# Block 2 of a hybrid transformer kernel: raw attention scores as three rounded products instead of one fp32 product

## The chip, the cores and the metric

The kernel runs on one core of one Trainium2 chip. The metric is the device time of one execution in microseconds (us). A core has a matrix engine (TensorE, PE in the rows, with its weight loads as PEld), a vector engine (VectorE, DVE), an activation engine (ScalarE, ACT), and a queue of DMA issues (SyncE, SP). Each works through its own list of instructions in order; they wait for each other by semaphores.

## The reference, cut to what matters

Four layers work on 512 tokens of width 1024 (`DEPTH = 2` layers of a first kind, then 2 of a second kind, "block 2"). Only block 2 is touched. Its layer is: one input projection, four groups of attention of four heads each with head width 64, an output projection, a layer norm, a gated feed-forward network, a layer norm. The four groups are

```python
out_a = _causal_softmax_blocks(fq, fk, fv, HEAD_DIM ** -0.5, cum)   # "FOX": causal, with a forget bias
out_b = _mla(cq, ckv, kr, ...)                                      # "MLA": q.k of 64 plus a rotary part of 32
out_c = _stick_breaking_blocks(sq, sk, sv)                          # "SB"
out_d = _swa_sink_alibi(wq, wk, wv, sinks, slopes)                  # "SWA": window of 128 keys
```

and each begins with raw scores s = q k^T over 64 channels, in fp32. These raw scores are all that the change is about.

## The kernel before, in words

**Data types.** A projection is not made with fp32 products. Each operand t is kept as a high part (t rounded to the type fp32r, made by a copy) and a rest (t minus the high part, again in fp32r), and a product is three rounded products, high x high, high x rest, rest x high, added up in PSUM: `mm3`, lines 583 to 587. ScalarE makes the high part of each weight unit (L1090), VectorE the rest (L1102). The raw scores of block 2 are the exception: their operands are plain fp32 tiles, and each is one fp32 product.

**The attention stage of block 2** has 32 steps in each of the two layers. Eight units of two heads follow each other (SWA, SWA, MLA, MLA, SB, SB, FOX, FOX), and each has four steps. Step s is unit a = s div 4, block qb = s mod 4. The two heads of a unit lie in one tile of 128 partitions, head 0 in partitions 0 to 63 and head 1 in 64 to 127. The names of the tiles are a letter for the kind (w, u, s, f for SWA, MLA, SB, FOX), q, k or v, and a number. `DEST` (L828) says where each lies.

**PE in step s**: the raw scores of step s (`scores`, L1932, product on L1943; for SB `sb_scores_of`, L1987, product on L1997), then weights times values of step s-2 (L1984, L2026), the transposes of the probabilities of step s-1 (L1968), and as filling the projection of later tiles in pieces of one eighth (`fill`, two halves a step; its order is `QUOTA`). In SB steps the running sums (L2012, L2015) stand in the place of the transposes, behind the first half of the filling. In step 8 (`FILL_FIRST`) the first half of the filling comes ahead of the scores. From step 28 on the scores are issued one step ahead. In the first step of a unit `operands_wait` (L1903) waits for the unit's q and k tiles. The number of key columns in one product is 128, 256, 384 and 512 in the four steps of a unit, in SWA 128, 256, 256 and 256.

**ACT in step s**: it copies the finished projection tiles out of PSUM (`tile_copy`, L2233), does what is due of v tiles and of norms (`rstd`, L2247, L2249), then the exponentials, then the copy of the transposed probabilities (L2279), and last the casts of weight units (`casts_of`, L1090).

**DVE in step s**: the row maxima (L761), the rests of weight units (L1102), the running sums of SB (L2610 to L2662), rotations (L2550 to L2552), the normalised query latents (L2568 to L2571, `query_latents`; the first in step 3, after `normalise`), `normalise` (L2537 to L2544), in step 7 the split of the rotated query (L2563, L2564), and in some steps a group norm or the sum of squares.

**When q and k tiles end.** A projection tile ends in the half step in which its last eighth is done (`ENDS`): wq1 in the second half of step 2, uq0 in the first half of 5, uk0 in the first half of 6, sq0 in the second of 7, uq1 and uk1 in the first of 8, sk0 in the second of 10, sq1 in the second of 14, sk1 in the second of 16, fq0 in the first of 19, fk0 in the second of 20, fq1 in the first of 23, fk1 in the second of 24. wq0 and wk are made ahead of step 0.

**DMA.** SP loads the weight units and, for MLA, exchanges halves of the rotary tiles (L956); the rotation of the query on DVE in step 7 (L2550) waits for these.

Of the kernel before, what the change touches and what calls it, by code (L numbers as in the profile page):

```python
# [35 lines left out]
SEQ = 512  # L36
# [72 lines left out]
class Steps:  # L109
# [10 lines left out]
    def wait(self, value=None):  # L120
# [12 lines left out]
          "sb_ln": 16, "sb_soft": 16, "sb_low": 12, "sb_cum": 16, "sb_sum": 12, "sb_prob": 16, "gate_ln": 1, "gate_ready": 1,  # L133
# [16 lines left out]
def program(nc, x_in, pos_in, const_in, mask_in, swa_in, rope2_in, col_in, w_in, row1_in,  # L150
            row2_in, out):
    ctx = ExitStack()
    with ctx:
# [110 lines left out]

        ps = [ctx.enter_context(nc.psum_tensor(f"bank{i}", [P, SEQ], F32)) for i in range(8)]
# [108 lines left out]
        gate_ln = sem("gate_ln")  # L374
        gate_in = sem("gate_in")
# [444 lines left out]
        def stacked(a, qb):  # L820
# [13 lines left out]
                "fv0": raw_t[0], "fv1": raw_t[1]}  # L834

# [1029 lines left out]
        def tensor_block2(pe, layer):  # L1865
# [67 lines left out]
            def scores(a, qb):  # L1933
# [4 lines left out]
                q, k = DEST[q_name(a)], DEST[k_name(a)]  # L1938
# [49 lines left out]
            def sb_scores_of(a, j):  # L1988
# [5 lines left out]
                q, k, S = DEST[q_name(a)], DEST[k_name(a)], banks(a, j)  # L1994
# [200 lines left out]
        def scalar_block2(act, st, layer):  # L2195
# [39 lines left out]

            def v_copy(name):
# [92 lines left out]
            for name in FIRST:  # L2329
                tile_copy(name)  # L2330
                next_cast(name)
            for step in range(STEPS):
                a, qb = divmod(step, NB)
                ended = ENDS.get((step - 1, 1), [])
                tiles_out(ended)
                late = LATE.get(step - 1, "")
# [35 lines left out]
                casts_of((*ended, *ENDS[step, 0]))  # L2372
            pT_copy(N_ATT - 1, NB - 1)
# [108 lines left out]
        def vector_block2(dve, st, layer):  # L2482
# [197 lines left out]

            for name in FIRST:
                next_split(name)
            for step in range(STEPS):
# [61 lines left out]
                if step == GATE_STEP + 1:  # L2745
                    gate_sums()
                if step == TAIL:
# [338 lines left out]
```

## Time and profile before

| | |
|---|---|
| Median of 3 runs | 2331.2 us (2330.55 to 2332.4) |
| Profiled execution, its own time | 2330.97 us |
| Its span from the first to the last instruction | 2329.2 us |
| Busy share of the span: PE, PEld, DVE, ACT | 99%, 81%, 63%, 42% |
| Granted clock of PE, mean | 0.999 |
| Chain that ended last, by engine | PE 98%, DVE 1%, ACT 1% |
| Attention stage of block 2, step 0 to the end of the scores of step 31 | about 1134.5 to 1316 us, and 1738 to 1920 us |

The chain of waits goes back from the last instruction to whatever released it. It gives a piece the time from the end of the piece before it, so a line of it is the time that the piece really took of the span, while the duration of a single matmul record holds the latency of a pipelined instruction. Matmuls on the same line that follow each other are one piece with their count. An fp32 product has two records, a rounded product has one, so a pair of heads in fp32 is "x4".

### The profile page before, as it was taken

How to read it: one execution, taken by the hardware profiler on the slowest of the kernel's cores; microseconds unless marked ns; L12 is line 12 of the kernel's file. 1: busy time of each engine (PE TensorE's matmuls, PEld its weight loads, DVE VectorE, ACT ScalarE, POOL GpSimd, SP SyncE). 2: the span in 40 equal slices, each digit the busy share in tenths (PEclk: the TensorE clock that was granted, in tenths of full speed). 3: DMA queues.
4: the chain of work that ended last, by engine and by line, in shares of the span. 5: the costliest groups of instructions: out<-in, count | busy, mean ns of one | idle time of the engine just before them, and what ended most of it. 6: DMA issues, size and time to landing. Idle time of an engine off the chain costs nothing.

```text
span 2329.2 us, 30258 instructions
## 1 busy us (share of the span) xinstructions
PE 2317.0 (99%) x11444; PEld 1879.2 (81%) x11444; DVE 1478.3 (63%) x2773; ACT 983.4 (42%) x1853; POOL 0.2 (0%) x4
## 2 busy tenths in 40 slices
PE   9999999999999999999999999999999999999998
PEld 7888888888888888888877788888887768888887
DVE  6788764345578774334577668567566767658565
ACT  5356542223446643222566533133246664323222
POOL 0000000000000000000000000000000000000000
PEclk9999999999999999999999999999999999999999
DMA  5333333332243333233231232324303112422322
GB/s 175 108 105 105 103 100 91 99 104 87 91 116 106 104 93 123 92 100 109 66 86 55 64 129 90 127 64 136 127 31 94 55 46 100 145 82 91 128 72 90
DMA packets 73583, 226.32 MB, mean 97 GB/s; under 512 B 14240, under 2 KB 15136, under 8 KB 72672
## 3 DMA queue, kind: packets, MB, share of 16 engines
q1 hardware_dynamic: 73296, 224.13, 30.9%
q8 instruction: 92, 1.51, 0.3%
q14 instruction: 51, 0.42, 0.1%
q10 hardware_dynamic: 144, 0.26, 0.0%
HBM read 204.83 MB, written 2.10 MB: 89 GB/s over the span
## 4 chain that ended last, share of the span: by engine, by line
PE 98%; DVE 1%; ACT 1%; DMA 0%; issue 0%; DVEq 0%
PE bank L585 26%; PE bank L587 25%; PE bank L586 25%; PE bank L2162 2%; PE bank L2161 2%; PE bank L2160 2%; PE bank L1256 2%; PE bank L1984 1%; PE bank L1943 1%; PE bank L1243 1%; PE bank L1968 1%; PE bank L519 1%; PE bank L1233 1%; PE bank L1231 1%; PE bank L1997 1%; PE bank L2026 0%
## 5 line engine op out<-in xcount | busy, mean ns | idle before, releaser
L585 PE MATMUL bank<-h_hi,w_hi 128*128 128x512 f32 x1984 | 787.7, 397 | 0.4 <-DVE w_lo L1102 0.2
L587 PE MATMUL bank<-h_lo,w_hi 128*128 128x512 f32 x1984 | 774.0, 390 | 0.0
L586 PE MATMUL bank<-h_hi,w_lo 128*128 128x512 f32 x1984 | 773.7, 390 | 0.0
L585 PEld LDWEIGHTS bank<-h_hi,w_hi 128*128 128x128 f32 x1984 | 373.0, 188 | 81.3 <-issue 7.5
L587 PEld LDWEIGHTS bank<-h_lo,w_hi 128*128 128x128 f32 x1984 | 372.5, 188 | 79.4
L586 PEld LDWEIGHTS bank<-h_hi,w_lo 128*128 128x128 f32 x1984 | 373.3, 188 | 71.4 <-issue 0.2
L1102 DVE TENSOR_TENSOR w_lo<-raw_w,w_hi 128x1024 fp32r<-128x1024 f32 x314 | 379.1, 1222 | 76.3 <-ACT w_hi L1090 73.2
L1090 ACT ACTIVATE w_hi<-raw_w 128x1024 fp32r<-128x1024 f32 x314 | 327.6, 1055 | 140.6 <-DMA raw_w<-w_dram 140.4
L2392 ACT ACTIVATE nrm<-bank 128x512 f32<-128x512 f32 x44 | 26.3, 599 | 288.7 <-PE bank L587 288.7
L1545 ACT ACTIVATE ext<-bank 128x512 f32<-128x512 f32 x48 | 28.7, 598 | 281.1 <-PE bank L587 281.1
L1845 DVE TENSOR_TENSOR rope_a<-ext,bank 128x512 f32<-128x512 f32 x32 | 22.0, 688 | 160.9 <-PE bank L587 107.4
L2160 PE MATMUL bank<-seven_hi,y_hi 128*128 128x512 f32 x252 | 98.1, 389 | 0.0
L2161 PE MATMUL bank<-seven_hi,y_lo 128*128 128x512 f32 x252 | 98.1, 389 | 0.0
L1489 ACT ACTIVATE prob<-prob,small 128x128 f32<-128x128 f32 (+3 forms) x128 | 70.9, 556 | 55.7 <-DVE small L761 55.7
L2774 DVE TENSOR_TENSOR ytmp<-nrm,bank 128x512 f32<-128x512 f32 x26 | 17.9, 687 | 117.3 <-PE bank L587 117.2
L585 PE MATMUL bank<-act_hi,w_hi 128*128 128x512 f32 x212 | 83.1, 392 | 0.0
L587 PE MATMUL bank<-act_lo,w_hi 128*128 128x512 f32 x212 | 82.6, 390 | 0.0
L586 PE MATMUL bank<-act_hi,w_lo 128*128 128x512 f32 x212 | 82.5, 389 | 0.0
L761 DVE CUSTOM_DVE_ANT_0 prob<-bank,causal 128x128 f32<-128x128 f32 (+3 forms) x112 | 49.4, 479 | 45.9 <-PE bank L1233 20.0
L2774 DVE TENSOR_TENSOR y_raw<-nrm,bank 128x512 f32<-128x512 f32 x18 | 12.4, 688 | 91.1 <-PE bank L587 91.1
L1502 ACT ACTIVATE pT<-bank 128x128 f32<-128x128 f32 (+3 forms) x96 | 38.2, 432 | 73.9 <-PE bank L1243 73.9
L2842 DVE SCALAR_TENSOR_TENSOR x<-x,bank 128x512 f32<-128x512 f32 x84 | 54.9, 686 | 20.8 <-PE bank L2162 20.8
(369 smaller groups left out, 3517.3 us busy)
## 6 DMA issues: line engine op xcount, KB each, us to landing
raw_w<-w_dram SPq DMA_DIRECT2D x312, 512.0 KB, 3.6
down_raw<-w_dram SPq DMA_DIRECT2D x36, 512.0 KB, 4.4
extra_raw<-w_dram SPq DMA_DIRECT2D x10, 512.0 KB, 4.6
k_lo<-k_lo SPq DMA_DIRECT2D x32, 128.0 KB, 2.3
ln_row<-row_dram SPq DMA_DIRECT2D x4, 1024.0 KB, 6.1
last_raw<-w_dram SPq DMA_DIRECT2D x8, 512.0 KB, 4.5
x<-x_dram SPq DMA_DIRECT2D x4, 512.0 KB, 6.9
rowp<-row_dram SPq DMA_DIRECT2D x2, 1024.0 KB, 9.1
```

What stands on the lines that cost most here:

```text
L585: nc.tensor.matmul(dst, lh, rh, start=start, stop=False)
L586: nc.tensor.matmul(dst, ll, rh, start=False, stop=False)
L587: return nc.tensor.matmul(dst, lh, rl, start=False, stop=stop)
L761: return nc.vector.tensor_tensor_reduce(out=to, in0=bank, in1=mask, scale=-1.0, scalar=3.0e38, op0=ALU.add, op1=ALU.min, accum_out=low)
L1090: nc.scalar.activation(hi_of(u), raw_of(u), ACT.Copy).then_inc(hi_cast, 1)
L1102: nc.vector.tensor_tensor(lo_of(u), raw_of(u), hi_of(u).bitcast(F32), ALU.subtract) \
L1256: last = nc.tensor.matmul(O[rows, cols], vs[a % 2][:, b, rows], pT[ti1(a, qb, m) % 2][:, b * P:(b + 1) * P], start=(b == 0), stop=(b == qb))
L1489: nc.scalar.activation(prob[m][:, 0:nk], prob[m][:, 0:nk], ACT.Exp, scale=-1.0, bias=small[:, 24 + 2 * qb + m:25 + 2 * qb + m], accum_out= ...
L2160: nc.tensor.matmul(bank[t][:, :], y_hi[:, p, a, y], high, start=begin, stop=False, skip_group_check=True)
L2161: nc.tensor.matmul(bank[t][:, :], y_lo[:, p, a, y], high, start=False, stop=False, skip_group_check=True)
L2162: made = nc.tensor.matmul(bank[t][:, :], y_hi[:, p, a, y], low, start=False, stop=p == PAIRS - 1, skip_group_check=True)
L2842: nc.vector.scalar_tensor_tensor(out=part, in0=part, scalar=scale, in1=bank[t][:, :], op0=ALU.mult, op1=sign).then_inc(down_added, 1)
```

## The change

Each q and k tile of the raw scores, in its place as fp32, gets a high part in another buffer (`HEAD_HIGH`) by a copy on ScalarE (`head_cast`), and its rest, written over the fp32 tile itself, by a subtraction on VectorE (`head_rest`). PE then makes three rounded products for each head, with the heads alternating. The casts stand at the end of an ACT step; for wq1 right behind the copy of the tile at the head of step 3. The rests stand at the end of the DVE step after the one in which the cast is due; for wq1 at the end of the same step 3. `operands_wait` also waits for the later one of the two rests.

```diff
+        HEAD_HIGH = {"wq0": act_hi[:, 0, :], "wk": act_hi[:, 1, :], "wq1": act_hi[:, 2, :], "uq0": act_lo[:, 7, :],
+                     "uk0": act_lo[:, 11, :], "sq0": spare[:, :], "uq1": act_hi[:, 8, :], "uk1": act_hi[:, 9, :],
+                     "sk0": act_hi[:, 10, :], "sq1": act_lo[:, 10, :], "sk1": act_lo[:, 11, :], "fq0": act_hi[:, 8, :],
+                     "fk0": act_hi[:, 9, :], "fq1": act_lo[:, 8, :], "fk1": act_lo[:, 9, :]}
...
+        HEAD_TURN = {name: i + 1 for i, name in enumerate(HEAD_HIGH)}
@@ tensor_block2
             def operands_wait(a):
                 tile_wait(q_name(a))
                 tile_wait(k_name(a))
+                if q_name(a) in HEAD_HIGH:
+                    pe.wait_ge(head_low, at(head_low, max(HEAD_TURN[q_name(a)], HEAD_TURN[k_name(a)])))
...
-                for m in range(2):
-                    bank_wait(a, qb, m)
-                    rows = slice(HD * m, HD * m + HD)
-                    last = nc.tensor.matmul(S[m][:, 0:nk], q[rows, block_q], k[rows, k0:k1], start=True, stop=(kind == SWA))
-                    if kind == SWA:
-                        last.then_inc(scores_ready, 1)
+                for i, (q, k) in enumerate(((q_hi, k_hi), (q_hi, k_low), (q_low, k_hi))):
+                    for m in range(2):
+                        if i == 0:
+                            bank_wait(a, qb, m)
+                        rows = slice(HD * m, HD * m + HD)
+                        last = nc.tensor.matmul(S[m][:, 0:nk], q[rows, block_q], k[rows, k0:k1],
+                                                start=(i == 0), stop=(kind == SWA and i == 2))
+                        if kind == SWA and i == 2:
+                            last.then_inc(scores_ready, 1)
...
-                for m in range(2):
-                    rows = slice(HD * m, HD * m + HD)
-                    nc.tensor.matmul(S[m][:, lo:SEQ], k[rows, lo:lo + P], q[rows, lo:SEQ], start=True, stop=True) \
-                      .then_inc(sb_scores, 1)
+                for i, (q, k) in enumerate(((q_hi, k_hi), (q_low, k_hi), (q_hi, k_low))):
+                    for m in range(2):
+                        rows = slice(HD * m, HD * m + HD)
+                        last = nc.tensor.matmul(S[m][:, lo:SEQ], k[rows, lo:lo + P], q[rows, lo:SEQ], start=(i == 0), stop=(i == 2))
+                        if i == 2:
+                            last.then_inc(sb_scores, 1)
@@ scalar_block2
+            def head_cast(name):
+                t = TILE[name]
+                if name in HEAD_HIGH:
+                    act.wait_ge(tile_out[t % 2], at(tile_out[t % 2], t // 2 + 1))
+                    nc.scalar.activation(HEAD_HIGH[name], DEST[name][:, :], ACT.Copy).then_inc(head_high, 1)
...
             for name in FIRST:
                 tile_copy(name)
+                head_cast(name)
                 next_cast(name)
...
                 tiles_out(ended)
+                if "wq1" in ended:
+                    head_cast("wq1")
...
                 casts_of((*ended, *ENDS[step, 0]))
+                for name in (*ended, *ENDS[step, 0]):
+                    if name != "wq1":
+                        head_cast(name)
@@ vector_block2
+            def head_rest(name):
+                if name in HEAD_HIGH:
+                    dve.wait_ge(head_high, at(head_high, HEAD_TURN[name]))
+                    nc.vector.tensor_tensor(head_parts(name)[1], DEST[name][:, :], HEAD_HIGH[name].bitcast(F32), ALU.subtract) \
+                      .then_inc(head_low, 1)
...
             for name in FIRST:
                 next_split(name)
+                head_rest(name)
...
                     gate_sums()
+                for name in (*ENDS.get((step - 2, 1), []), *ENDS.get((step - 1, 0), []), *ended):
+                    if (name == "wq1") == (name in ended):
+                        head_rest(name)
```

`head_parts(name)` is the pair of the high part and the rest. The biases that are added to the scores in PSUM (L1949, L1954, L1959) and all else are left as they are.

## Rows read from the trace of the kernel before

**Rows 1.** The page: busy time by engine, and the last chain by engine.
```profile
PE 2317.0 (99%) x11444; PEld 1879.2 (81%) x11444; DVE 1478.3 (63%) x2773; ACT 983.4 (42%) x1853; POOL 0.2 (0%) x4
...
PE 98%; DVE 1%; ACT 1%; DMA 0%; issue 0%; DVEq 0%
```

**Rows 2.** Lines L1943 and L1997: durations in ns, starts, forms.
```profile
L1943 PE MATMUL bank<-ks,qs x128: 271/482/694, 1188.1 to 1918.6; 64*128 64x128 f32 x32, 64*128 64x256 f32 x32, 64*128 64x384 f32 x32, 64*128 64x512 f32 x32
...
L1943 PE MATMUL bank<-wk_t,wq_t x64: 271/377/481, 1134.5 to 1784.5; 64*128 64x256 f32 x48, 64*128 64x128 f32 x16
...
L1997 PE MATMUL bank<-wq_t,wk_t x32: 272/482/694, 1230.1 to 1854.1; 64*128 64x128 f32 x8, 64*128 64x256 f32 x8, 64*128 64x384 f32 x8, 64*128 64x512 f32 x8
...
L1997 PE MATMUL bank<-cq_t,ckv_t x32: 271/482/694, 1257.4 to 1882.2; 64*128 64x128 f32 x8, 64*128 64x256 f32 x8, 64*128 64x384 f32 x8, 64*128 64x512 f32 x8
```

**Rows 3.** Chain of waits, raw scores of 256, 128, 384, 512 columns: start, us, piece.
```profile
1180.42 0.63 PE bank L1943 x4
...
1188.16 0.42 PE bank L1943 x4
...
1196.65 0.85 PE bank L1943 x4
...
1202.50 1.06 PE bank L1943 x4
```

**Rows 4.** Chain of waits, two rounded bias products: 128, 256, 384, 512 columns.
```profile
1285.60 0.37 PE bank L1949 x2
...
1291.98 0.43 PE bank L1949 x2
...
1297.39 0.55 PE bank L1949 x2
...
1302.72 0.66 PE bank L1949 x2
```

**Rows 5.** Chain of waits, rounded products of block 1: 128, 256, 384, 512 columns.
```profile
110.29 0.22 PE bank L1233 x2
...
113.53 0.24 PE bank L1233 x2
...
119.71 0.36 PE bank L1233 x2
...
126.47 0.45 PE bank L1233 x2
```

**Rows 6.** Step 3 into 4, first layer: timelines of ACT, DVE; PE's chain.
```profile
1155.51 0.60 ACT L2247 ACTIVATE sz<-bank 128x512 f32<-128x512 f32 x1 [0.26 <-PE bank L1900]
...
1163.21 0.69 DVE L2571 TENSOR_TENSOR act_lo<-ytmp,act_hi 128x512 fp32r<-128x512 f32 x1
...
1162.77 0.42 PE bank L1943 x4
```

**Rows 7.** Step 7 into 8, both layers: timeline of DVE; PE's chain.
```profile
1184.73 0.69 DVE L2550 TENSOR_TENSOR rope_a<-raw_t,cos 128x512 f32<-128x512 f32 x1 [2.19 <-DMA nrm<-raw_t]
...
1189.31 0.69 DVE L2564 TENSOR_TENSOR act_lo<-qr_t,act_lo 128x512 fp32r<-128x512 f32 x1
...
1792.18 0.69 DVE L2564 TENSOR_TENSOR act_lo<-qr_t,act_lo 128x512 fp32r<-128x512 f32 x1
...
1792.02 0.42 PE bank L1943 x4
```

**Rows 8.** Steps 19 to 23, first layer: window of step 19; DVE's timeline; PE's chain.
```profile
1249.90:1257.50 7.60, 7.60 (x38) 5.38 (x40) 7.36 (x19) 6.41 (x12) 0.00 (x0) 1.00 0.22 69
...
1273.62 0.43 DVE L2662 TENSOR_TENSOR sp_low<-pn,act_hi 128x256 fp32r<-128x256 f32 x1
...
1274.99 0.29 PE bank L2012 x2
...
1281.65 0.56 DVE L2662 TENSOR_TENSOR sp_low<-ext,act_hi 128x384 fp32r<-128x384 f32 x1
...
1282.50 0.37 PE bank L2012 x2
```

More of the change, by code:

```diff
@@ L132 @@
           "pv_done": 32, "o_out": 8, "sq_ready": 6, "sq_parts": 5, "rs_ready": 6, "y_ready": 8, "sb_scores": 16, "sb_masked": 16,
-          "sb_ln": 16, "sb_soft": 16, "sb_low": 12, "sb_cum": 16, "sb_sum": 12, "sb_prob": 16, "gate_ln": 1, "gate_ready": 1,
+          "sb_ln": 16, "sb_soft": 16, "sb_low": 12, "sb_cum": 16, "sb_sum": 12, "sb_prob": 16, "gate_ln": 1, "gate_ready": 1, "head_high": 15, "head_low": 15,
           "latent_ready": 3, "gu_ready": END_TILES, "pair_ready": 2 * PAIRS * SEVEN_PARTS, "down_done": 14 * SEVEN_PARTS,
@@ L263, in program @@
         last_hi = [sb(f"last_hi{i}", [P, UNIT], F32R, at=at[1]) for i, at in enumerate(last_at)]
+        head_rests = {name: sb(f"{name}_rest", [P, SEQ], F32R, at=addr[name])
+                      for name in ("wq_t0", "wq_t1", "wk_t", "ckv_t", "cq_t0", "qs0", "qs1", "ks0", "ks1")}
         ps = [ctx.enter_context(nc.psum_tensor(f"bank{i}", [P, SEQ], F32)) for i in range(8)]
@@ L374, in program @@
         gate_ln = sem("gate_ln")
+        head_high = sem("head_high")
+        head_low = sem("head_low")
         gate_in = sem("gate_in")
@@ L834, in program, with head_parts @@
                 "fv0": raw_t[0], "fv1": raw_t[1]}
+        HEAD_HIGH = {"wq0": act_hi[:, 0, :], "wk": act_hi[:, 1, :], "wq1": act_hi[:, 2, :], "uq0": act_lo[:, 7, :],
+                     "uk0": act_lo[:, 11, :], "sq0": spare[:, :], "uq1": act_hi[:, 8, :], "uk1": act_hi[:, 9, :],
+                     "sk0": act_hi[:, 10, :], "sq1": act_lo[:, 10, :], "sk1": act_lo[:, 11, :], "fq0": act_hi[:, 8, :],
+                     "fk0": act_hi[:, 9, :], "fq1": act_lo[:, 8, :], "fk1": act_lo[:, 9, :]}
+        HEAD_HOME = {"wq0": "wq_t0", "wk": "wk_t", "wq1": "wq_t1", "uq0": "qs0", "uk0": "ks0",
+                     "sq0": "wq_t0", "uq1": "qs1", "uk1": "ks1", "sk0": "wk_t", "sq1": "cq_t0",
+                     "sk1": "ckv_t", "fq0": "qs0", "fk0": "ks0", "fq1": "qs1", "fk1": "ks1"}
+        HEAD_TURN = {name: i + 1 for i, name in enumerate(HEAD_HIGH)}
+        def head_parts(name):
+            return HEAD_HIGH[name], head_rests[HEAD_HOME[name]][:, :]
         def q_name(a):
@@ L1937, in scores @@
                     operands_wait(a)
[L1938 removed]
+                (q_hi, q_low), (k_hi, k_low) = head_parts(q_name(a)), head_parts(k_name(a))
                 S = banks(a, qb)
[L1940 to L1945 removed]
+                for i, (q, k) in enumerate(((q_hi, k_hi), (q_hi, k_low), (q_low, k_hi))):
[7 more added lines that the diff above has]
+                            last.then_inc(scores_ready, 1)
                 for m in range(2):
@@ L1993, in sb_scores_of @@
                 bank_wait(a, j, 0)
-                q, k, S = DEST[q_name(a)], DEST[k_name(a)], banks(a, j)
-                for m in range(2):
-                    rows = slice(HD * m, HD * m + HD)
-                    nc.tensor.matmul(S[m][:, lo:SEQ], k[rows, lo:lo + P], q[rows, lo:SEQ], start=True, stop=True) \
-                      .then_inc(sb_scores, 1)
+                (q_hi, q_low), (k_hi, k_low), S = head_parts(q_name(a)), head_parts(k_name(a)), banks(a, j)
+                for i, (q, k) in enumerate(((q_hi, k_hi), (q_low, k_hi), (q_hi, k_low))):
[4 more added lines that the diff above has]
+                            last.then_inc(sb_scores, 1)
             def sb_between(a, j):
```

## The prediction
> **What bounds the kernel now.** I read the page first: PE is busy 99% of the span, and the chain that ended last is 98% PE [rows 1]. So whatever PE no longer does is gained one for one, and every time PE has to wait for a new thing is lost one for one; there is no slack on PE in which a wait could hide. DVE and ACT have slack on average, and the average says nothing here: what matters is whether DVE has finished at the moments at which PE asks. So I next read the scores' lines for how many products there are [rows 2], the chain of waits for what a pair of heads takes of the span [rows 3], and the timelines of DVE and ACT around the starts of units for when a rest could be ready [rows 6 to 8].
>
> **Part 1: the products on PE.** Counting records [rows 2] and dividing by 4 (two heads, two records each), both layers hold 16 pairs of 128 columns, 24 of 256, 12 of 384 and 12 of 512, 64 in all. They take 0.42, 0.63, 0.85 and 1.06 us [rows 3]. That is 0.21 us of lead-in and then 0.21 us for each 128 columns of both heads together. By the durations of the records [rows 2] each head of a pair of 512 columns needs some 0.85 us by itself, so the heads already run side by side in fp32, and this is not what the change brings.
>
> The three rounded pairs do not occur in this trace on half the rows. The nearest rows are two rounded products one after the other behind a change of the array's shape: 0.37, 0.43, 0.55 and 0.66 us [rows 4], lead-in included. A third one costs half of the rows for pairs in block 1, 0.11, 0.12, 0.18 and 0.225 us [rows 5]. If the two heads run side by side as they do in fp32, three pairs are therefore 0.48, 0.55, 0.73 and 0.885 us. The differences are +0.06, -0.08, -0.12 and -0.175 us, so 16 x 0.06 - 24 x 0.08 - 12 x 0.12 - 12 x 0.175 = **-4.5 us**. At 128 columns it is a loss, since a rounded product of 128 columns is no faster than 0.11 us. Bounds: if they do not overlap at all, each pair has three more products of 0.11 to 0.225 us, 16 x 0.33 + 24 x 0.36 + 12 x 0.54 + 12 x 0.675 = +28.5 us, so +24 us in place of -4.5. In the other direction, if the lead-in of about 0.2 us went away, 64 x 0.2 = 12.8 us more would be gained. I take -4.5, as side by side is what this trace shows of tiles of this shape.
>
> The skill bears on this twice. The Trainium skill, TensorEngine Tiling (Array Packing), Key Properties, says that different tiles load and multiply in parallel, and that a change of tiling mode drains the engine: that speaks for the overlap and for the lead-in staying. Against the full overlap stands the Trainium skill, TensorE: Matmul & The Clock Gate, Part 3, where four tiles packed by rows gave 3.07 times, not four times. With a loss of that proportion the sum would be higher by an estimated 8 us; the fp32 pairs of this trace show no such loss.
>
> **Part 2: the casts and rests.** 15 tiles in each of 2 layers give 30 casts on ACT and 30 rests on DVE. A rest is a 128x512 subtraction like L2571, 0.69 us [rows 6], 21 us of DVE in all; a cast is about as long as L2247, 0.60 us [rows 6], 18 us of ACT. Most of it lies beside PE's work. The casts of wq0 and wk, and their rests, are done about 1.3 us ahead of the scores of step 0. The rests of sq0, sk0, uq1, uk1, sq1, sk1, fq0 to fk1 are issued one to seven steps ahead of their use, so these waits cost nothing in themselves. Two rests have no step between them and their use, and these are the price of the change.
>
> **wq1, step 3 into 4.** Its rest is at the end of DVE's step 3, behind `query_latents(0)`, whose last instruction starts at 1163.21 and lasts 0.69 us, until 1163.9. PE begins the scores of step 4 at 1162.77 [rows 6], so DVE is already 1.1 us behind PE there; nobody waited for it before. The cast on ACT sits ahead of L2247, in an idle time of 0.26 us [rows 6]; it takes 0.5 us of issue and so moves ACT by 0.26, and with it the cast of a weight unit and all of DVE's step behind that. The rest ends at 1163.93 + 0.26 + 0.69 = 1164.9. PE stands for 2.1 us, in both layers: +4.2 us. Behind the waiting scores on PE are the weights times values of step 2, the transposes and the filling, all ready and all held up, as PE is in order.
>
> **uk0, step 7 into 8.** Its rest is at the end of DVE's step 7, behind the rotation of the query (which waits for a DMA until 1184.73), a weight unit's rest, `normalise` and the query's split. The last of these starts at 1189.31 and 1792.18; the next could start 0.61 us later and lasts 0.69, so it ends at 1190.6 and 1793.5. PE wants to start the scores of step 8 at 1188.16 [rows 3] and 1792.02 [rows 7]. That is 2.5 and 1.5 us, and PE comes 0.16 us earlier in each layer from its savings in steps 6 and 7, while the DMA keeps its time: +4.3 us. The cast of uk0 is done several us before. The rest of uq0, at the end of step 6, falls into DVE's idle time of 2.19 us ahead of the rotation [rows 7] and costs nothing. The three rests at the end of step 9 come when PE has been put back by 2 us, and are absorbed.
>
> **Steps 18 to 23, SB.** Here DVE has nearly no idle time: 7.36 of 7.6 us in step 19 [rows 8]. The casts of sk1 (ACT's step 17) and the rests of sk1, fq0 and fk0 (DVE's steps 18, 20, 22) put it back by 0.5 + 0.6 + 0.6 us before it next catches up. PE needs the low parts of SB's sums: the second of step 21 ends at 1274.05 and is used at 1274.99, that of step 22 ends at 1282.2 and is used at 1282.50 [rows 8]. Slack is 0.9 and 0.3 us, so 1.7 us of delay costs some 1.1 us at the first and 0.5 at the second, 1.6 us a layer; the second layer's DVE has a quarter us more of idle time. Bounds are 0 and 1.6 us; I take 1.2 a layer, nearer to the worked end, **+2.4 us**.
>
> **Sum:** -4.5 + 4.2 + 4.3 + 2.4 = +6.4 us. The profiled execution took 2330.97 us, which gives 2337.4; the median of the runs is 0.2 us above it, so 2337.5 us. A measurement of this kernel can tell about 0.2%, 4.7 us, from no change.
>
> **The rivals.**
> - *The SB stretch absorbs its rests.* PE's own savings or idle time of DVE that I have not seen hide them; only the waits for wq1 and uk0 are paid. 2331.0 - 4.5 + 8.5 = 2335.1 us, no change that can be told. For it: DVE's late times there were worked out through a long chain. Against: the slack of 0.3 us [rows 8]. 0.20.
> - *The two waits are not paid*, since DVE comes earlier than I worked out: 2331.2 - 4.5 = 2326.7, on the edge of faster. Against it: in both layers DVE is late already [rows 6, 7]. 0.06.
> - *The lead-in goes away (faster).* Rounded operands of the scores let PE load their weights beneath the projection product ahead of them, at the head of each of the 64 groups. Then 2337.5 - 12.8 = 2324.7 us. It decides from 0.18 us a group: 11 us bring it below 2326.5. Against it: the rounded products behind a change of shape pay about 0.2 us as well (0.66 us for two of 0.225) [rows 4, 5]. 0.06.
> - *Heads overlap only in part.* A loss of 0.04 us for each of the 192 rounded pairs is 8 us: 2345.5 us. The record of fp32 speaks against it [rows 3]. It is the packing figure of the Trainium skill, TensorE: Matmul & The Clock Gate, Part 3. 0.08.
> - *Rounded products of two heads don't overlap at all.* 2337.5 + 28.5 = 2366 us. Nothing in this trace shows rounded products on half the rows. 0.08.
> - *The change doesn't do what it says* is little of a rival here, as the instructions are counted; it would be that three rounded pairs take what two fp32 records took, with the waits paid: 2331.2 + 10.9 = 2342.1. 0.04.
>
> **How the numbers follow.** My forecast, 2337.5 us, has 0.48; its own range is 2334.5 to 2341. The cases from 2335.1 to 2345.5 hold 0.80 together; the range runs from 2331 (taking in that both the waits and the SB stretch cost less) to 2345. Slower by over 0.2% (above 2335.9) is most of the forecast and the three dearer cases: 0.42 + 0.08 + 0.08 + 0.04 = 0.62. Within 0.2%: the first rival, the forecast's lower end and half of the second: 0.29. Faster: 0.09.
>
> **What would show it.** In the profile after, the score groups in the chain should read x6 and 0.48, 0.55, 0.73 and 0.89 us. PE should have a wait of 2.1 us on `head_rest` ahead of step 4's scores in each layer, and of 2.7 and 1.7 us ahead of step 8's, and these should be the longest waits of PE. L2012 should be released by DVE's L2662 in steps 22 and 23. PE's busy time should fall a little, and DVE's and ACT's rise by some 20 us each. I am wrong if the groups are above 1 us at 256 columns (no overlap), if the two waits are under 1 us, or if PE's idle time is elsewhere.

## The result, and the profile after

| | before | after |
|---|---|---|
| Median of the runs | 2331.61 us (2330.55 to 2332.4, 4 runs) | 2344.91 us (2341.99 to 2347.39, 4 runs) |
| Ratio | | 1.0058, 95% interval 1.0046 to 1.007 |
| Profiled execution, its own time | 2330.97 us | 2347.39 us |
| Its span | 2329.2 us | 2345.6 us |
| Granted clock of PE, mean | 0.999 | 0.996 |

The changed kernel is slower by 13.3 us. The forecast was 6.3 us slower, 2337.5 us, in a range that ended at 2345.0: the sign is right and the median just inside, but the size is wrong by more than a factor of two. That the median lies inside is luck: no case on which the range was built holds what makes up the difference. The profiled execution is the slowest of the four, by 2.5 us over the median; why will be seen below.

The page of the kernel after, busy time by engine and the last chain by engine (against [rows 1]):

```profile
PE 2321.6 (99%) x11572; PEld 1892.3 (81%) x11572; DVE 1496.7 (64%) x2803; ACT 999.1 (43%) x1883; POOL 0.2 (0%) x4
...
PE 92%; DVE 4%; ACT 2%; issue 1%; SPq 1%; DMA 1%; DVEq 0%; ACTq 0%
```

DVE has 30 instructions and 18.4 us more, ACT 30 and 15.7 us more. PE's share of the last chain has gone from 98% to 92%. PE's busy time has risen by 4.6 us, although each large group has become shorter. That is the first sign of something that the forecast does not contain.

The chain of waits of the kernel after, raw scores of 256, 384, 512 and 128 columns (against [rows 3]):

```profile
1147.79 0.55 PE bank L1965 x6
...
1205.09 0.72 PE bank L1965 x6
...
1210.81 0.89 PE bank L1965 x6
...
1216.98 0.48 PE bank L1965 x6
```

Forecast were 0.55, 0.73, 0.885 and 0.48 us. The products cost what was worked out.

PE's waits in the kernel after: total us, times, longest. All that stands here is new; in the same view of the kernel before, no wait lies on a line of the raw scores or of SB's sums.

```profile
PE bank L1965 <- DVE wq_t_rest L2721: 4.7, 2, 2.4
PE bank L1965 <- issue: 2.6, 1, 2.6
PE bank L1965 <- ACT ks L2258: 2.0, 1, 2.0
...
PE bank L2037 <- DVE sp_low L2699: 0.7, 4, 0.2
...
PE bank L1991 <- DVE pn L2581: 0.6, 1, 0.6
```

L1965 is the raw scores' product, L2721 the rest. The first row is the wait for wq1's rest ahead of step 4, in both layers. The second and third are the waits ahead of step 8. "ACT ks" had been copied long before, so this is a case in which the view names the wrong releaser; the timelines of DVE and PE show the right one:

```profile
1163.52 0.69 DVE L2608 TENSOR_TENSOR act_lo<-ytmp,act_hi 128x512 fp32r<-128x512 f32 x1
1164.25 0.69 DVE L2721 TENSOR_TENSOR wq_t_rest<-wq_t,act_hi 128x512 fp32r<-128x512 f32 x1
...
1165.20 0.33 PE L1965 MATMUL bank<-act_hi 64*128 64x128 f32 x2 [2.35 <-DVE wq_t_rest L2721]
...
1194.25 0.68 DVE L2721 TENSOR_TENSOR ks_rest<-ks,act_lo 128x512 fp32r<-128x512 f32 x1
...
1195.14 0.33 PE L1965 MATMUL bank<-act_lo 64*128 64x128 f32 x2 [1.97 <-ACT ks L2258]
```

The rest of wq1 ends at 1164.94, the forecast said 1164.9; PE goes on 0.26 us later, which the forecast had left out. The rest of uk0 ends at 1194.93, and PE goes on at 1195.14.

What follows each of the four waits is the surprise. The windows of the kernel after, 3.3 or 3.4 us each, which begin 0.4 to 2.2 us after PE has gone on (columns: us; busy time of PE, PEld, DVE, ACT, POOL; PEclk, the granted clock; DMA share; GB/s):

```profile
1166.50:1169.90 3.40, 3.40 (x11) 2.83 (x10) 3.24 (x7) 1.56 (x8) 0.00 (x0) 0.51 0.00 0
1197.30:1200.60 3.30, 3.30 (x12) 2.16 (x11) 2.26 (x6) 3.30 (x8) 0.00 (x0) 0.50 0.54 120
1777.50:1780.90 3.40, 3.40 (x20) 2.70 (x19) 3.00 (x10) 1.97 (x8) 0.00 (x0) 0.51 0.04 16
1808.20:1811.60 3.40, 3.40 (x15) 2.68 (x12) 2.02 (x10) 3.06 (x9) 0.00 (x0) 0.51 0.33 80
```

The same place in the kernel before, where PE had not waited:

```profile
1162.80:1166.20 3.40, 3.40 (x25) 2.77 (x26) 3.19 (x11) 3.39 (x11) 0.00 (x0) 1.00 0.50 154
```

PE's clock falls from 2.4 to 1.2 GHz for some 3.4 us behind each wait. PE counts as fully busy in these windows, so no view of waits shows the loss. The chain shows it as twice the price of the same product:

```profile
1153.64 0.23 PE bank L591
...
1168.55 0.42 PE bank L590
1168.98 0.43 PE bank L591
1169.40 0.43 PE bank L592
```

To follow where the time goes, I took from the timelines when the scores of a step begin, relative to the scores of step 0 of the first layer, and the difference to the kernel before. A rise from one row to the next is time lost there. The columns of the runs are explained with them; "again" is a second profile of the changed kernel.

```
layer, step  after  again  E3 both  E4 all  E9 fp32  E10 cast
1       3    -0.11  -0.11   -0.11   -0.11    0.00    -0.11
1       4     2.23   2.23   -0.19   -0.19    0.00    -0.19
1       5     3.91   3.85   -0.13   -0.13    0.00    -0.13
1       7     4.09   4.08    0.09    0.09    0.29    -0.32
1       8     6.78   7.05    0.35    0.63    0.47     0.57
1       9     8.02   7.11    0.41    0.69    0.72     0.63
1      22     7.43   6.20   -0.52   -0.39    0.83    -0.42
1      24     8.69   7.46    0.73   -0.20    0.87    -0.24
1      31     8.22   6.99    0.25   -0.67    0.86    -0.71
2       3     7.95   6.77    0.02   -0.91    0.87    -0.95
2       4    10.29   9.11   -0.07   -0.99    0.87    -1.03
2       5    11.87   9.15   -0.01   -0.93    0.87    -0.97
2       7    12.07   9.35    0.17   -0.71    1.17    -1.16
2       8    14.73  11.97    0.13   -0.76    1.17    -1.20
2       9    16.34  13.60    0.19   -0.70    1.17    -1.14
2      22    15.54  12.83   -0.61   -1.64    1.17    -2.09
2      24    16.77  14.04    0.59   -1.47    1.13    -1.92
2      31    16.30  13.57    0.12   -1.94    1.13    -2.39
```

In the column "after" each wait shows as two steps: the wait itself (2.34 us from step 3 to 4, 2.69 us from 7 to 8), and then 1.68, 1.24, 1.58 and 1.61 us in the step behind it, 6.1 us in all. Between steps 22 and 24, SB, 1.26 and 1.23 us are lost. Elsewhere the shift falls slowly, which is the saving of the products.

### The profile page after: what moved, and what is told of

Read it like the earlier page. It is cut to its first block, busy times and chain, and to the rows that moved or that the text cites. A ratio compares the mean times of both kernels' runs of the same rounds, so it can differ in the third digit from the quotient of the medians.

```text
span 2345.6 us, 30586 instructions
## 1 busy us (share of the span) xinstructions
PE 2321.6 (99%) x11572; PEld 1892.3 (81%) x11572; DVE 1496.7 (64%) x2803; ACT 999.1 (43%) x1883; POOL 0.2 (0%) x4
## 4 chain that ended last, share of the span: by engine, by line
PE 92%; DVE 4%; ACT 2%; issue 1%; SPq 1%; DMA 1%; DVEq 0%; ACTq 0%
PE bank L590 24%; PE bank L592 24%; PE bank L591 24%; PE bank L2187 2%; PE bank L2185 2%; PE bank L2186 2%; PE bank L1274 2%; PE bank L2007 1%; PE bank L1261 1%; PE bank L1991 1%; PE bank L1965 1%; PE bank L524 1%; PE bank L1251 1%; PE bank L1249 1%; DVE w_lo L1120 1%
```

## The experiments

The theory at this point, **C**: the forecast's steps are right, and what it lacks is a price for the half clock behind each of the two waits in each layer. The rival, **R**: the clock falls for the load of the added work and not for the waits; when a wait is taken away, its own length alone comes back.

**E1, the rest of wq1 forward,** right behind the row maxima of step 3:

```diff
                     row_max(a, qb, 1)
+                if "wq1" in ended:
+                    head_rest("wq1")
...
-                    if (name == "wq1") == (name in ended):
+                    if name not in ('wq1',) and (name == "wq1") == (name in ended):
```

> Only the rest of wq1 is moved, from the end of DVE's step 3 to right behind its two row maxima, where DVE stands idle for 2.7 us and the cast is long done. Theory C (a wait of PE costs its own length and, behind it, a stretch of 3.4 us at half clock, 1.7 us): 2344.9 - 2 x 2.35 - 2 x 1.7 = 2336.8 us, two stretches at a clock of 0.5 in place of four, none behind step 4. Rival R (the clock falls for the load of the added work and not for the waits; only the waits themselves come back): 2340.2 us, and the clock still falls near 1167 us. By both PE has no wait above 0.3 us ahead of step 4's scores.

Measured: 2338.45 us (8 runs), ratio 1.0029 [1.0018, 1.0039]. It lies between both expectations and decides nothing by itself. PE has no wait at step 4 any more; those at step 8 stay. The timeline of PE and the windows behind the two waits of this kernel:

```profile
1189.83 0.33 PE L1965 MATMUL bank<-act_lo 64*128 64x128 f32 x2 [1.82 <-ACT ks L2258]
...
1795.56 0.33 PE L1965 MATMUL bank<-act_lo 64*128 64x128 f32 x2 [2.03 <-ACT ks L2258]
```

```profile
1191.50:1194.80 3.30, 3.30 (x26) 2.31 (x27) 2.49 (x7) 3.30 (x11) 0.00 (x0) 1.00 0.46 104
1797.20:1800.50 3.30, 3.30 (x10) 2.37 (x9) 2.26 (x6) 3.26 (x11) 0.00 (x0) 0.50 0.43 83
```

In this profile the wait of the second layer has the half clock behind it, that of the first has not. So the price does not come with every wait; a single profile cannot give it.

**E2, the rest of uk0 forward,** in step 7 ahead of the query's rotation, that of wq1 as in the changed kernel:

```diff
+                if "uk0" in ENDS.get((step - 1, 0), []):
+                    head_rest("uk0")
                 if LATE.get(step - 2) == "cq":
                     query_latents(1)
```

> Only the rest of uk0 is moved, from the end of DVE's step 7 to ahead of the rotation of the query, where DVE waits 0.85 us for a DMA. Theory C: two waits of 2.6 us and two stretches at half clock go: 2344.9 - 5.2 - 3.4 = 2336.3 us, with no fall of the clock behind step 8. Rival R: 2339.7 us, the clock still falls near 1197 us.

Measured: 2339.66 us (4 runs), 1.0036 [1.0022, 1.005]: the time that R expected. But the fall of the clock near 1197 us that R expected too is not there; the profile shows C's mechanism with a size that C did not have. The waits at step 8 are gone, the two of 2.36 us at step 4 remain, and behind the first the clock is half for twice as long:

```profile
1165.30:1171.90 6.60, 6.60 (x28) 5.28 (x29) 4.69 (x14) 1.94 (x8) 0.00 (x0) 0.50 0.05 22
1776.20:1779.50 3.30, 3.30 (x9) 2.52 (x9) 3.13 (x7) 1.11 (x6) 0.00 (x0) 0.50 0.00 0
```

From step 4 to 5 the long one costs 3.1 us (the shift, taken as in the table, goes from 2.23 to 5.35 us) and the short one 1.7 us (7.58 to 9.24).

**E3, both forward:**

> Both moves together. Theory C: 2344.9 - 4.7 - 5.2 - 6.8 = 2328.2 us, below the kernel before (2331.6), clock 0.999 as before, and only the SB stretch's late low parts (about 1.3 us a layer) left of the cost. Rival R: 2335.0 us, slower than before, clock 0.996.

Measured: 2331.58 us (11 runs), ratio 1.0000 [0.9991, 1.0009]. The two moves, of two subtractions of 0.69 us per layer, give back all that the change had cost: 13.3 us of median. There is no stretch of half clock in the attention stage, and PE has no wait on L1965, although every cast and rest is still made. R falls. C's time missed by 3.4 us: it took four stretches of 1.7 us off a median of executions that do not all have four (E11 below). What is still lost stands in the column "E3 both" of the table. Between steps 22 and 24 it loses 1.25 and 1.20 us, and from step 5 to 9 of the first layer 0.54 us.

**E4, the SB stretch relieved as well.** To test whether the first of these is the rests of sk1, fq0 and fk0, they stand between DVE's softplus sums, sk1 and fk0 ahead of the second, fq0 ahead of the first:

```diff
+                if "fq0" in ENDS.get((NB * a + j - 2, 0), []):
+                    head_rest("fq0")
                 for m in range(2):
+                    if m and "sk1" in ENDS.get((NB * a + j - 2, 1), []):
+                        head_rest("sk1")
+                    if m and "fk0" in ENDS.get((NB * a + j - 3, 1), []):
+                        head_rest("fk0")
                     dve.wait_ge(sb_ln, at(sb_ln, w + m + 1))
```

> As the one before, and in the SB steps the rests of sk1, fq0 and fk0 are moved from the ends of DVE's steps 18, 20 and 22 into places where it waited for ACT: between the two softplus sums of steps 18 and 23, and ahead of them in step 21. Theory S (these three rests made the low parts of the SB sums late): the loss of 1.3 us a layer at steps 22 to 24 goes, 2325.5 us. Rival (the late part comes from the casts on ACT in steps 17 and 19, or DVE is simply full): 2328 us, L2037 in the same wait.

Measured: 2329.02 us (11 runs), 0.999 [0.9981, 0.9999]. 2.6 us faster than E3, and 2.5 us faster than the kernel before. The steps 22 to 24 now lose 0.19 and 0.17 us. So the rests of SB cost 2.6 us with everything else equal. The second low part of steps 21 and 22 on DVE's timeline, E3 and then E4, against 1273.62 and 1281.65 us before [rows 8]:

```profile
1274.32 0.43 DVE L2699 TENSOR_TENSOR sp_low<-pn,act_hi 128x256 fp32r<-128x256 f32 x1
...
1282.35 0.56 DVE L2699 TENSOR_TENSOR sp_low<-ext,act_hi 128x384 fp32r<-128x384 f32 x1
```

```profile
1273.53 0.43 DVE L2705 TENSOR_TENSOR sp_low<-pn,act_hi 128x256 fp32r<-128x256 f32 x1
...
1281.56 0.56 DVE L2705 TENSOR_TENSOR sp_low<-ext,act_hi 128x384 fp32r<-128x384 f32 x1
```

In E3 they come 0.70 us late, in E4 0.09 us early. PE comes to step 22 of E3 0.5 us early, by its shorter products, and loses that and 0.7 us more. The view of waits shows two waits of 0.2 us there in the profile of E3, one in each layer, and two in that of E4 as well; the difference lies in gaps too short for the view. Three rests that PE asks for only steps later cost 1.3 us a layer, by what stands behind them in DVE's list. The time that theory S gave, 2325.5 us, stood on C's 2328.2 us for E3; its step of 2.6 us was right.

**E5, the wait covered instead of taken away.** The rest of wq1 stays late, but PE gets ready work ahead of the scores of step 4:

```diff
-                if step == FILL_FIRST:
+                if step in (4, FILL_FIRST):
...
-                if step != FILL_FIRST:
+                if step not in (4, FILL_FIRST):
```

> The changed kernel with every cast and rest where it was, but PE's filling of step 4 that stood behind that step's first scores is issued ahead of them (some 2.1 us of ready work against the wait of 2.35 us for the rest of wq1). Theory C (what the wait costs is PE standing still, plus a stretch at half clock behind it): PE's wait ahead of step 4's scores is 0.3 us or gone, no half clock behind it, and the time is near that of the kernel with wq1's rest moved forward, 2338.5 us (2337 to 2340.5). Rival R (the late rest puts back the chain of DVE and ACT behind it, so that filling in PE's gap only moves the gap into the steps after it): PE's idle time comes back in steps 4 to 6 and the time stays above 2342 us.

Measured: 2340.26 us (4 runs), 1.0038 [1.0023, 1.0053], inside C's range and 1.8 us above E1, whose waits at step 8 were shorter. PE waits 0.32 us instead of 2.35. The rows, waits at step 4 and twice at step 8, and the windows behind those at step 8:

```profile
1166.16 0.33 PE L1965 MATMUL bank<-act_hi 64*128 64x128 f32 x2 [0.32 <-DVE wq_t_rest L2721]
...
1192.08 0.33 PE L1965 MATMUL bank<-act_lo 64*128 64x128 f32 x2 [2.24 <-ACT ks L2258]
...
1798.52 0.33 PE L1965 MATMUL bank<-act_lo 64*128 64x128 f32 x2 [2.33 <-ACT ks L2258]
```

```profile
1193.80:1197.10 3.30, 3.30 (x26) 2.30 (x26) 2.53 (x7) 3.30 (x11) 0.00 (x0) 1.00 0.55 138
1798.80:1805.50 6.70, 6.70 (x35) 4.77 (x32) 3.33 (x11) 4.63 (x11) 0.00 (x0) 0.50 0.36 90
```

At the scores of step 5 this kernel is 0.24 us behind the kernel before, where the changed kernel is 3.91 behind. The rival, that the loss only moves into the steps behind, had 2342 us or more and falls. So the late rest by itself costs little; it is PE standing still that costs, and where PE did not stand, the clock stayed full. At step 8, the wait of 2.33 us had a long half clock behind it and the one of 2.24 us none.

**E6, the products undone, all else kept.** Raw scores as before's two fp32 products; the rests go over the high parts and nobody reads them:

```diff
-                for i, (q, k) in enumerate(((q_hi, k_hi), (q_hi, k_low), (q_low, k_hi))):
-                    for m in range(2):
...
+                for m in range(2):
+                    bank_wait(a, qb, m)
+                    rows = slice(HD * m, HD * m + HD)
+                    last = nc.tensor.matmul(S[m][:, 0:nk], q[rows, block_q], k[rows, k0:k1], start=True, stop=(kind == SWA))
...
-                    nc.vector.tensor_tensor(head_parts(name)[1], DEST[name][:, :], HEAD_HIGH[name].bitcast(F32), ALU.subtract) \
+                    nc.vector.tensor_tensor(HEAD_HIGH[name], DEST[name][:, :], HEAD_HIGH[name].bitcast(F32), ALU.subtract) \
```

> The changed kernel with all its casts, rests and waits, but the raw scores as the two fp32 products of before; the rests are written over the high parts and are read by nobody. It isolates the products. Theory P (three rounded pairs cost 0.48, 0.55, 0.72 and 0.89 us where fp32 costs 0.42, 0.63, 0.85 and 1.06): the waits of 2.35 and 2.6 us stay, the groups are those of before, and the time is that of the changed kernel, 2344.9 us, plus 4 to 5 us: 2349.3 us (2347.5 to 2351.5). Rival: the saving of the products is lost again elsewhere (PE only waits longer for DVE or the exchange), and the time is within 1.5 us of the changed kernel's.

Measured: 2347.31 us (4 runs), 1.0068 [1.0051, 1.0084], 16.1 us above the kernel before of the same chip, where the changed kernel was 13.3 above. The waits and the half clock are there with fp32 products too (2.27, 2.66, 2.27 and 1.32 us, the first three followed by half clock in this profile), so they do not belong to the rounded products. The saving comes out at 2.8 us instead of 4 to 5, between both expectations, but the number of half-clock stretches varies from run to run and blurs such a difference. E9 is the cleaner price.

**E7, the heads not in turn.** On E4: all three products of one head, then all three of the other.

```diff
-                for i, (q, k) in enumerate(((q_hi, k_hi), (q_hi, k_low), (q_low, k_hi))):
-                    for m in range(2):
+                for m in range(2):
+                    for i, (q, k) in enumerate(((q_hi, k_hi), (q_hi, k_low), (q_low, k_hi))):
```

> The fastest version so far (all five rests moved forward, 2329.0 us) with the three rounded products of one head ahead of the three of the other, in place of the two heads in turn. Theory 1 (only neighbours of different heads run side by side: of six products one pair overlaps, so a group takes two products more, 0.22, 0.24, 0.36 and 0.45 us): 16 x 0.22 + 24 x 0.24 + 12 x 0.36 + 12 x 0.45 = 19 us more, 2348 us (2344 to 2352). Theory 2 (PE takes the products of the second head beside the first's whatever their order): 2329 to 2331 us. Theory 3 (nothing overlaps): 28.5 us more, 2357.5 us.

Measured: 2329.12 us (10 runs), 0.9991 [0.9982, 1.0]. No difference to E4's 2329.02; theory 2 holds, and the alternation brings nothing. The timeline of PE of this kernel, a group of 128 columns, puts one product of each head (x2) at each start, although in the program the three of the first head come first:

```profile
1208.96 0.33 PE L1965 MATMUL bank<-act_hi 64*128 64x128 f32 x2
1209.12 0.28 PE L1965 MATMUL bank<-ks_rest,act_hi 64*128 64x128 f32 x2
1209.24 0.28 PE L1965 MATMUL bank<-act_hi,qs_rest 64*128 64x128 f32 x2
```

The trace has the second head's first product 10 ns behind the first head's first, not behind its third. The Trainium skill, TensorEngine Tiling (Array Packing), Key Properties, says that different tiles can load and multiply in parallel; the trace agrees, and adds that a tile does not wait for products that are ahead of it in the program but on the other rows. In all 64 groups of this profile the second head starts 10 ns behind the first. So "PE is in order", as the forecast has it, holds for the waiting scores and what stands behind them, and not between the two heads' products.

**E8, a shorter wait.** wq1's rest forward, uk0's rest between step 7's `normalise` and the query's split:

```diff
+                if "uk0" in ENDS.get((step - 1, 0), []):
+                    head_rest("uk0")
                 if ROTATE2.get(step - 1) == "qr":
                     dve.wait_ge(qk_ready, at(qk_ready, 2))
                     split_query()
```

> The rest of wq1 moved forward as before, that of uk0 only ahead of the query's split at the end of step 7, so that PE's wait for it ahead of step 8 is some 1.0 to 2.0 us in place of 2.0 to 2.7; none at step 4. Theory C (every such wait is followed by a stretch of half clock worth 1.6 us): 2331.6 + 2 x 1.5 + 2 x 1.6 = 2337.8 us. Rival L (a wait clearly shorter than 2 us leaves the clock full; in the runs so far waits of 2.35 and 2.7 us were always followed by half clock and one of 2.0 us was not): 2331.6 + 2 x 1.5 = 2334.6 us, and no stretch at half clock in the profile.

Measured: 2333.84 us (10 runs), 1.0013 [1.0003, 1.0022]. PE's waits at step 8:

```profile
1189.35 0.33 PE L1965 MATMUL bank<-act_lo 64*128 64x128 f32 x2 [0.93 <-ACT ks L2258]
...
1794.52 0.33 PE L1965 MATMUL bank<-act_lo 64*128 64x128 f32 x2 [1.41 <-issue]
```

No half clock in the profile, as L expected, and 2333.84 us is nearer to its 2334.6 than to C's 2337.8; E3 + 0.9 + 1.4 gives 2333.9. But of the ten runs seven lie between 2332.3 and 2333.9 us and three at 2336.0 to 2336.9, and two of these three have a mean clock of 0.998 where the others have 0.999. Only one run is profiled, so what these three did is not seen; a half-clock stretch would fit them. A wait of 1 to 1.4 us is cheaper; that it is safe is not shown.

**E9, the products priced without disturbance:** E4 with the fp32 products, edited as in E6.

> All casts and rests of the fastest version (all five rests moved forward), but the raw scores as the two fp32 products of before; the rests are written over the high parts and read by nobody. It prices the products where no long wait and no half clock blur it, and the casts and rests where no product uses them. Theory P (the saving of 4.5 us is gained in full, and casts and rests cost 2.0 us beside it): 2329.0 + 4.5 = 2333.5 us (2332.7 to 2334.3). Rival A (a part of the saving is eaten, since PE, come earlier, waits longer for DVE, ACT or the exchange in steps 5 to 8 and 20 to 23; with long waits kept, the fp32 version was slower than the changed kernel by only 2.4 us): 2331.4 us (2331.0 to 2332.2).

Measured: 2332.72 us (11 runs), 1.0005 [0.9996, 1.0014]: on the lower edge of P's range, nearer to P than to A. Against the kernels before of their own chips, E9 is 1.3 us slower and E4 2.5 us faster, so the products bring 3.8 us. The table shows where a part of the 4.5 goes: in the waitless steps 9 to 22 of the first layer E4 gains 1.08 us, where the forecast's differences give 1.03; but in steps 22 to 24, where the groups alone would gain 0.30 us more in each layer, E4 loses 0.15 and 0.21 us on E9. PE, come earlier, meets DVE there. Another 0.3 us in the first layer and 0.1 us in the second go between steps 5 and 9, where E4 gains less on E9 than the groups alone give. That is 1.3 us lost in these two profiles, where the medians show 0.7; the products bring between 3.2 and 3.8 us. And the 1.3 us of E9 are the price of casts and rests with nothing moved wrongly, 0.83 us of it in steps 5 to 10 of the first layer and 0.30 in the second.

**E10, one cast moved.** In E4, DVE's rotation in step 6 starts when its exchange lands, at 1179.16 us against 1178.12 before. ACT's new cast of uq0 stands just ahead of the copy that feeds the exchange, so I moved it into ACT's idle time of step 6:

```diff
+                if "uk0" in ENDS[step, 0]:
+                    head_cast("uq0")
                 if "uv0" in ENDS[step, 0]:
                     tile_copy("uv0")
...
-                    if name != "wq1":
+                    if name not in ("wq1", "uq0"):
```

> The fastest version with ACT's cast of uq0 taken from the end of step 5, where it stands ahead of the copy that feeds the exchange of the rotated halves (DVE got them at 1179.16 us in place of 1178.12), into ACT's idle time of 1.9 us in step 6. Theory X (this cast makes the exchange late, and that makes PE lose some 0.3 us in step 6 and 0.5 us in step 7, in the first layer, and 0.3 us in the second): the exchange lands near 1178.2 us and the time is 2328.0 us (2327.5 to 2328.5). Rival: the exchange's landing is set by other DMAs on the queues, and the time stays at 2329.0 us.

Measured: 2328.95 us (11 runs), 0.9989 [0.998, 0.9998], the same as E4. The theory falls. The copy is back where it was before (1175.99 us, before 1175.96), and the exchange lands late all the same, here on DVE's timeline:

```profile
1179.23 0.69 DVE L2589 TENSOR_TENSOR rope_a<-raw_t,cos 128x512 f32<-128x512 f32 x1 [1.22 <-DMA rope_b<-raw_t]
```

PE is 0.4 us earlier at step 7. In the first layer it loses that by step 8: its wait for the normalised probabilities (L1991) is 0.87 us in place of 0.52, so the gain was swallowed by the next thing that is late. In the second layer this profile keeps its 0.4 us, which the medians do not show. Why the exchange lands later than before remains open.

**E11, the changed kernel again,** for more runs and a second profile:

> The changed kernel once more, unchanged, for more runs of it and a second profile. If each half-clock stretch of 3.41 us behind a wait costs some 1.6 us and may fail to come or come twice as long, the runs spread by more than those of kernels without such waits (1.7 us): from about 2341 to 2348 us, median 2343 to 2346 us; the waits themselves (2.35 us at step 4 of both layers, 2.0 and 2.6 us at step 8) are the same in the second profile to 0.1 us, and only the number or length of the stretches behind them differs. If instead the stretches belong to the kernel and not to the execution, the second profile has the same four and the time is 2347 us again.

Measured: 2344.44 us (4 runs, 2343.14 to 2345.97), 1.0056 [1.0042, 1.007]. The waits at step 4 are those of the first profile, that at step 8 of the first layer is not: 2.82 us in place of 1.97. PE's four waits in this profile, and the windows behind them:

```profile
1164.45 0.33 PE L1965 MATMUL bank<-act_hi 64*128 64x128 f32 x2 [2.36 <-DVE wq_t_rest L2721]
...
1194.65 0.33 PE L1965 MATMUL bank<-act_lo 64*128 64x128 f32 x2 [2.82 <-ACT ks L2258]
...
1775.18 0.33 PE L1965 MATMUL bank<-act_hi 64*128 64x128 f32 x2 [2.36 <-DVE wq_t_rest L2721]
...
1803.42 0.33 PE L1965 MATMUL bank<-act_lo 64*128 64x128 f32 x2 [2.59 <-issue]
```

```profile
1166.20:1169.50 3.30, 3.30 (x9) 2.52 (x9) 3.13 (x7) 1.12 (x6) 0.00 (x0) 0.50 0.00 0
1196.40:1199.70 3.30, 3.30 (x28) 2.29 (x26) 2.55 (x7) 3.30 (x10) 0.00 (x0) 1.00 0.59 113
1776.90:1780.20 3.30, 3.30 (x17) 2.69 (x16) 3.13 (x7) 1.15 (x6) 0.00 (x0) 1.00 0.00 0
1804.50:1807.80 3.30, 3.30 (x16) 2.68 (x15) 1.75 (x9) 2.58 (x8) 0.00 (x0) 0.50 0.37 89
```

This is the cleanest pair of the study. The wait of 2.36 us at step 4 is the same in both layers, and so is the work behind it. In the first layer the clock falls and the scores of step 5 come 1.62 us late on top of the wait (3.85 - 2.23); in the second it does not fall, and the step costs 0.04 us (9.15 - 9.11). So the half clock costs 1.6 us, it is caused by nothing in the program that differs between the two, and it does not always come. The execution with this profile took 2343.96 us with two stretches, the first one 2347.39 with four. Less 1.6 us for each, they give 2340.8 and 2341.0 us.

Over all profiles of these runs, 17 waits of PE of 1.8 to 2.9 us stand ahead of raw scores, and 13 are followed by half clock, 11 times some 3.4 us long and twice some 6.8. The four without are of 1.82, 2.24, 2.36 and 2.82 us, so between 1.8 and 2.9 us the length does not decide it. Of the three between 0.9 and 1.4 us none is. In none of the 13 profiles does the clock fall anywhere else before PE's last product, as far as it is recorded (from 4 to 8 us on). PE's waits of 1.1 to 1.3 us on L524, some 8 us behind the start in E2, E3, E6 and E10, have none behind them either.

## Why the prediction was wrong

The account of the changed kernel, each term from a difference of medians against the kernel before on the same chip, or from the two profiles:

| term | forecast | measured | from |
|---|---|---|---|
| products | -4.5 | -3.8 | E9 against E4; 3.2 by the steps of the profiles |
| other casts and rests | 0 | +1.3 | E9 against before |
| rests in SB | +2.4 | +2.6 | E3 against E4 |
| the two waits per layer | +8.5 | +9.3 | 2340.9, less E3 |
| half clock behind them | none | +3.9 | the rest, 13.3 less the terms above; in the two profiles 6.1 and 3.2 by the steps |
| sum | +6.4 | +13.3 | |

The last two terms were parted by the price of 1.6 us for a stretch. The lengths of the waits in the two profiles add up to 9.9 us, with the 0.6 us for the probabilities, and to 10.1 us; by these the half clock has 3.1 to 3.3 us in the median.

- **The failing step** is that of the two waits: "every time PE has to wait for a new thing is lost one for one". The first layer's wait for wq1 was forecast as 2.1 us and measured 2.35, ending where it was said to (the rest at 1164.9). What failed is "one for one". The half clock is 3.9 us of the 6.9 by which this sum missed, or 3.1 by the lengths of the waits, the largest part either way. A wait of 2.0 to 2.8 us cost 1.6 us more for each stretch of half clock behind it, twice that if it was long. The sum had no term for the clock, and neither had the range nor a rival. The trace of before could not price it, as it holds no wait of PE above 1.4 us in this stage or elsewhere. But it held a warning. At the end of the program PE's last product begins at 2320.87 us and lasts 0.39, and 2.4 us after its end the clock is at half (columns as above):

```profile
2320.00:2323.60 3.60, 1.25 (x6) 0.71 (x4) 2.24 (x5) 1.30 (x3) 0.00 (x0) 1.00 0.36 146
2323.70:2329.00 5.30, 0.00 (x0) 0.00 (x0) 2.38 (x3) 0.25 (x2) 0.00 (x0) 0.50 0.51 198
```

A forecast that lets PE stand for 2.1 to 2.7 us should have had a rival with a fall of the clock in it.
- **What the waits are long by.** At step 8 the forecast had 2.66 and 1.66 us; measured were 2.0 us with 0.6 us for the probabilities ahead of it in the first layer, 2.82 in the second profile, and 2.6 us in the second layer. The forecast said that PE comes earlier and "the DMA keeps its time", with the absolute times of the trace before. In fact everything had been put back by 4 us by step 7. In E1, where nothing is put back ahead of step 8, the two waits were 1.82 and 2.03 us, so the forecast's first was too long and its second too short even there; why was not traced.
- **The products** were right group by group: 0.48, 0.55, 0.72 and 0.89 us. That they came to 3.8 us instead of 4.5 is a small loss to the statement that whatever PE no longer does "is gained one for one": ahead of a place where DVE is late, the gain is taken back.
- **The SB stretch** was right in its sum, 2.6 against 2.4 us, and in its mechanism: the rests make DVE's low parts late, and PE waits for them at L2037. The rival that it absorbs them falls, by E4. The size is in part luck. DVE was to be 1.7 us late and was 0.70 (E3). Against that the slack was too large: PE waits for the low part already ahead of the product with the high part, which begins at 1274.83 and 1282.34 us, so before it was 0.79 and 0.14 us and not 0.9 and 0.3, and PE came 0.5 us earlier by its savings, which the forecast left out here.
- **Casts and rests that "cost nothing"** cost 1.3 us, 1.1 of it in steps 5 to 10. Which of them costs it is not shown. The exchange for the rotation of step 6 lands 1 us later than before, but the one cast that was moved for it (E10) changed neither that nor the time.
- **The other rivals.** The waits were paid (E1, E2, E3). The lead-in stayed: 0.48 us at 128 columns. No partial or missing overlap: the groups, and E7, in which the other order of the products took the same time. Partial overlap had 2345.5 us, close to the result, by a mechanism that does not act; it is also counted into the 0.80 of the range, though it lies above the range's end of 2345. The first rival's 2335.1 is 2335.0 by its own terms.
- Of what I said would show it, PE's busy time should have fallen a little and rose by 4.6 us: the four stretches at half clock lengthened it, and without them, in E3, it is 2.3 us below the kernel before (2314.7 us). This line of the page was the quickest hint that the clock had a part.

## What to carry to other kernels

When a change adds a dependency to the engine that bounds the kernel, look for the two or three places where the new operand is asked for right after it is made, and put exactly those first on the engine that makes it; here two subtractions of 0.69 us per layer in the wrong place cost 13.3 us, and the other new casts and rests some 4 us together, 2.6 of it by three rests. In this kernel, price a wait of PE of 2 us or more at its length plus 1.6 us, with a range of 0 to 3.2, and let the window behind it, by granted clock, tell you afterwards. If the producer cannot be moved, independent work of PE ahead of the waiting product does the same (E5). The change with its five early rests, E4, is the version to keep: 2329.02 us, 0.1% below the kernel before, with an interval that ends at 0.01%.

## What the runs showed of the hardware

- The granted clock fell to half behind waits of PE as short as 2.03 us (E1), for some 3.4 or some 6.8 us, at 1.6 or about 3.1 us of cost, and not every time: the same wait of 2.36 us in the same execution had it once and once not (E11). The Trainium skill, TensorE: Matmul & The Clock Gate, Why this matters for your kernels, ties the loss to idle gaps of PE longer than any that occurred here ahead of a product (2.82 us, E11); these runs do not agree, and the measurement decides.
- Three rounded products for each of two heads take the same time in both orders tried, in turn or head by head; the second head's product started 10 ns behind the first's across two products issued between them (E7).
- Three rounded products for each of two heads, on half the rows each, cost 0.48, 0.55, 0.72 and 0.89 us for 128 to 512 columns against 0.42, 0.63, 0.84 and 1.06 us for fp32 in the same place (E6). At 128 columns the rounded form is the dearer one.
